# Weight sums of the seven-product pairs moved to GpSimd, part sums kept in PSUM, low parts merged

## The chip, the cores and the metric

The kernel runs on one core of a Trainium2 chip. The metric is the device time of one execution in microseconds, the median of several runs. The profile is of one further execution on the same core, taken by the hardware profiler.

## The reference

One inference step of a decoder trunk with two layers, on 576 tokens (64 sample tokens and 512 prompt tokens) of 1024 features. Each layer is a feed-forward block a, a token mixer (mLSTM in layer 0, gated linear attention in layer 1) and a feed-forward block b:

```python
x = x + 0.5 * swiglu(rmsnorm(x, norm_w[l, 0]), w_gate, w_up, w_down)
x = x + mixer(rmsnorm(x, norm_w[l, 1]))
x = x + 0.5 * swiglu(rmsnorm(x, norm_w[l, 2]), w_gate, w_up, w_down)

def swiglu(x, w_gate, w_up, w_down):
    return (silu(x @ w_gate) * (x @ w_up)) @ w_down
```

Everything is float32 in and out. The hidden width is 2816, that is 22 tiles of 128. The change touches the four feed-forward blocks.

## The kernel before

All features lie on partitions; x, the weights and the hidden rows are held in tiles of 128 features, and the 576 tokens are two halves of 288 columns (FIRST and SECOND). A float32 product is made on TensorE from three fp32r products, high times high, high times low and low times high. So each weight block that arrives by DMA in `raw` is rounded to `w_hi` by ScalarE (ACT), and VectorE (DVE) subtracts to make `w_lo`. `raw`, `w_hi` and `w_lo` have four slots of 1024 columns; a pair (a gate block and an up block for the same 128 hidden features) takes slots 0 and 1 or slots 2 and 3 (half 0 and half 1), and PSUM banks 0 to 3 or 4 to 7.

`schedule` (L35) lays out the phases. Each feed-forward block has three G phases (8, 8 and 6 pairs; `GROUPS`, L20), and each is followed by a D phase (4 pairs) that multiplies the hidden tiles by `w_down` and adds to x. In group 0 the first five pairs are plain: 96 matmuls of 288 columns each (`feature_pair`, L502). The last three pairs of group 0 and all pairs of groups 1 and 2 are seven-product pairs (`seven_pair`, L523): gate and up weights, over even and odd feature tiles, and the two token halves are taken as a two-by-two matrix product, which needs seven half-size products in place of eight, 84 matmuls. There are 17 such pairs in a block and 68 in all. The price is sums: of x (`th_hi`, `th_lo`, made once a block by `u_sums` L1895 and `t_sums` L1919), of weights (S1 to S4: `sum_3`, `sum_1`, `sum_2`, `sum_4`, L1771 to L1798, all on DVE), their high and low parts (`unit_high` L1198 and `unit_low` L1766, 512 columns each), and of products.

The products P1 to P7 of a pair run in a fixed order (L552 to L568). Product sums go like this before: ACT copies bank b+1 to SBUF after P1, P3 and P5 (`product_copy` L1217), and DVE adds these copies to banks in four steps (`part`, L1808), which leave the gate row in `T(0)` and bank b+1, and the up row in `T(1)`. Then come silu (L1252, L1254; in group 0 after a multiplication by `rstd`, `rows_scale` L1812, then L1257), the product of gate and up (`rows_product` L1822), and its high and low parts into `h_hi`, `h_lo`.

The order on each engine is written out by hand and each engine runs its instructions in order. On DVE the body of a seven-product pair w is `seven_pair` (L1842): between its own low parts and part sums it finishes the rows of pair w-1 and makes the weight sums of pair w+1. On ACT it is `seven_rest` (L1228) and `seven_rows` (L1246), which call `seven_start` (L1221) of the pair after. SyncE (SP) issues every weight load; the load of a slot waits on `lo_done` (L356), that is for the low part of what the slot held. GpSimd (POOL) has only small work in the mixers (L1710 to L1733).

`T(i)` is one of ten scratch rows of 576 columns. `bc` (L151) holds rows that the mixers broadcast. `own` makes DVE wait for its own last instruction.

## Time and profile before

| | |
|---|---|
| median of 3 runs | 2196.25 us (2194.16 to 2197.27) |
| span of the profiled execution | 2198.8 us |
| busy PE, DVE, ACT, POOL | 2160.5, 1555.5, 951.1, 45.7 us |
| matmuls | 16360, of which 5712 in seven-product pairs (L536) |
| chain that ended last | PE 91%, DVE 5%, ACT 2% |
| PE idle, from first to last matmul and before | some 29 us in gaps of over 0.05 us, 8.9 of it before the first matmul |

PE is TensorE's matmuls, PEld its weight loads, PEclk the granted clock in tenths of full speed. Matmuls are pipelined: a record of one lasts 0.29 us while they start some 0.13 us apart, so a stage is read by where it begins and ends, not by the busy time of a group. In a timeline, a record's end overlaps the start of the next on the same engine; the distance from start to start is what an instruction costs its engine.

### The profile page before, as it was taken

How to read it: one execution, taken by the hardware profiler on the slowest of the kernel's cores; microseconds unless marked ns; L12 is line 12 of the kernel's file. 1: busy time of each engine (PE TensorE's matmuls, PEld its weight loads, DVE VectorE, ACT ScalarE, POOL GpSimd, SP SyncE). 2: the span in 40 equal slices, each digit the busy share in tenths (PEclk: the TensorE clock that was granted, in tenths of full speed). 3: DMA queues.
4: the chain of work that ended last, by engine and by line, in shares of the span. 5: the costliest groups of instructions: out<-in, count | busy, mean ns of one | idle time of the engine just before them, and what ended most of it. 6: DMA issues, size and time to landing. Idle time of an engine off the chain costs nothing.

```text
span 2198.8 us, 40702 instructions
## 1 busy us (share of the span) xinstructions
PE 2160.5 (98%) x16360; PEld 2137.4 (97%) x16360; DVE 1555.5 (71%) x2379; ACT 951.1 (43%) x1495; POOL 45.7 (2%) x50
## 2 busy tenths in 40 slices
PE   7999999999999999999999999999999999999997
PEld 7999999999999999999999999999999899999997
DVE  6898657685555798848679984863776457988485
ACT  5435435454433444515445452544322434445252
POOL 0000000001100000000000000000011100000000
PEclk9999999999999999999999999999999999999999
DMA  5222322224332232222323232232122222223222
GB/s 186 68 88 95 115 67 86 96 82 137 99 118 85 68 102 82 95 87 89 104 70 94 86 96 96 82 101 94 44 96 84 97 77 84 90 87 104 77 86 73
DMA packets 72578, 201.58 MB, mean 92 GB/s; under 512 B 7268, under 2 KB 26980, under 8 KB 72448
## 3 DMA queue, kind: packets, MB, share of 16 engines
q1 hardware_dynamic: 72448, 199.80, 28.1%
q8 instruction: 88, 1.44, 0.3%
q14 instruction: 42, 0.34, 0.1%
HBM read 187.82 MB, written 11.95 MB: 91 GB/s over the span
## 4 chain that ended last, share of the span: by engine, by line
PE 91%; DVE 5%; ACT 2%; issue 1%; DMA 0%; POOL 0%; SPq 0%; DVEq 0%; POOLq 0%
PE ps L479 48%; PE ps L536 32%; PE ps L753 4%; PE ps L608 1%; DVE w_lo L1768 1%; PE ps L784 1%; PE ps L773 1%; PE ps L787 0%; DVE w_lo L1753 0%; PE ps L803 0%; PE ps L617 0%; PE ps L796 0%; PE ps L631 0%; PE ps L797 0%; DMA x<-in_x 0%
## 5 line engine op out<-in xcount | busy, mean ns | idle before, releaser
L479 PE MATMUL ps<-h_lo,w_hi 128*128 128x288 f32 x1616 | 347.0, 294 | 4.1 <-DVE h_hi L2267 4.1
L479 PE MATMUL ps<-h_hi,w_hi 128*128 128x288 f32 x1616 | 346.5, 294 | 0.7 <-DVE w_lo L1753 0.7
L536 PE MATMUL ps<-th_hi,w_hi 128*128 128x288 f32 x1088 | 320.2, 294 | 2.4 <-ACT scratch L1219 2.4
L536 PE MATMUL ps<-th_lo,w_hi 128*128 128x288 f32 x1088 | 320.9, 295 | 0.0
L536 PE MATMUL ps<-th_hi,w_lo 128*128 128x288 f32 x1088 | 319.8, 294 | 0.0
L479 PE MATMUL ps<-h_hi,w_lo 128*128 128x288 f32 x1360 | 290.2, 292 | 0.0
L479 PE MATMUL ps<-xn_hi,w_hi 128*128 128x288 f32 x1152 | 257.2, 300 | 11.6 <-DVE w_lo L1753 8.9
L479 PEld LDWEIGHTS ps<-h_lo,w_hi 128*128 128x128 f32 x1616 | 259.9, 188 | 4.8 <-DVE h_hi L2267 4.5
L479 PEld LDWEIGHTS ps<-h_hi,w_hi 128*128 128x128 f32 x1616 | 259.9, 188 | 1.0 <-DVE w_lo L1753 0.9
L1753 DVE TENSOR_TENSOR w_lo<-raw,w_hi 128x1024 fp32r<-128x1024 f32 x196 | 232.2, 1221 | 36.9 <-ACT w_hi L1185 35.1
L479 PE MATMUL ps<-xn_hi,w_lo 128*128 128x288 f32 x1152 | 251.9, 296 | 0.0
L479 PE MATMUL ps<-xn_lo,w_hi 128*128 128x288 f32 x1152 | 251.7, 296 | 0.0
L1768 DVE TENSOR_TENSOR w_lo<-scratch,w_hi 128x512 fp32r<-128x512 f32 x272 | 181.8, 690 | 84.8 <-ACT w_hi L1200 84.4
L1185 ACT ACTIVATE w_hi<-raw 128x1024 fp32r<-128x1024 f32 x196 | 195.8, 1047 | 105.2 <-PE ps L479 80.5
L536 PE MATMUL ps<-xn_hi,w_lo 128*128 128x288 f32 x816 | 240.4, 295 | 0.0
L536 PE MATMUL ps<-xn_hi,w_hi 128*128 128x288 f32 x816 | 239.9, 294 | 0.0
L536 PE MATMUL ps<-xn_lo,w_hi 128*128 128x288 f32 x816 | 239.9, 294 | 0.0
L479 PEld LDWEIGHTS ps<-h_hi,w_lo 128*128 128x128 f32 x1360 | 217.5, 187 | 0.0
L536 PEld LDWEIGHTS ps<-th_hi,w_hi 128*128 128x128 f32 x1088 | 204.8, 188 | 3.7 <-issue 3.2
L479 PEld LDWEIGHTS ps<-xn_hi,w_hi 128*128 128x128 f32 x1152 | 187.7, 190 | 19.9 <-issue 17.5
L2019 DVE SCALAR_TENSOR_TENSOR x<-ps,x 128x1152 f32<-128x1152 f32 x52 | 70.5, 1356 | 191.9 <-PE ps L479 191.9
L536 PEld LDWEIGHTS ps<-th_hi,w_lo 128*128 128x128 f32 x1088 | 204.4, 188 | 0.0
(288 smaller groups left out, 4119.7 us busy)
## 6 DMA issues: line engine op xcount, KB each, us to landing
raw<-in_w_gate SPq DMA_DIRECT2D x88, 512.0 KB, 3.4
raw<-in_w_up SPq DMA_DIRECT2D x88, 512.0 KB, 4.2
raw<-in_w_down SPq DMA_DIRECT2D x64, 512.0 KB, 3.6
raw<-in_w_mix SPq DMA_DIRECT2D x64, 512.0 KB, 4.2
raw<-in_w_down SPq DMA_DIRECT2D x32, 384.0 KB, 3.2
state_s<-in_state_c SPq DMA_DIRECT2D x4, 1024.0 KB, 7.5
out_c_s<-state_s SPq DMA_DIRECT2D x4, 1024.0 KB, 4.6
state_s<-in_state_g SPq DMA_DIRECT2D x4, 1024.0 KB, 6.1
```

Of the source, the lines that this page charges most:

```text
L479: ins = nc.tensor.matmul(o, a, b[:, c] if c is not None else b, start=first and j == 0, stop=last and j == 2)
L536: ins = nc.tensor.matmul(ps[:, bank, FIRST], left, b_, start=first and k == 0 and j == 0, stop=k == KT_X // 2 - 1 and j == 2, skip_group_c ...
L608: ins = nc.tensor.matmul(ps[:, bank, c * P:(c + 1) * P], left[:, ts], right[:, ts], start=True, stop=True)
L753: ins = nc.tensor.matmul(out, a[:, k, xs], b[:, 2 * half:2 * half + 2, ws], start=k == 0 and j == 0, stop=k == KT_X - 1 and j == 2)
L773: ins = nc.tensor.matmul(ps[:, 4 + c // 2, (c % 2) * DV:(c % 2 + 1) * DV], k_tok[:, c, :], v_tok[:, 1 + c, h * DV:(h + 1) * DV], start=Tru ...
L784: ins = nc.tensor.matmul(out, v_tok[:, 1 + c, vs], att(mixer, h)[:, c * P:(c + 1) * P], start=True, stop=c == 0)
L1185: nc.scalar.activation(w_hi[:, slot, :], raw[:, slot, :], ACT.Copy).then_inc(hi_done, 1)
L1753: V.tensor_tensor(w_lo[:, slot, :], raw[:, slot, :], w_hi[:, slot, :].bitcast(f32), ALU.subtract).then_inc(lo_done, 1)
L1768: return V.tensor_tensor(by_tile(unit(w_lo, half, u)), src, by_tile(unit(w_hi, half, u)).bitcast(f32), ALU.subtract)
L2019: ins = V.scalar_tensor_tensor(xs, ps[:, b:b + 4, 0:HALF_TOK], scale, xs, ALU.mult, ALU.add)
```

## The change

Weights. The host stores the gate and up weights of a pair so that four units of 512 columns lie one after the other: W12 and W11 (gate, odd and even feature tiles), then W21 and W22 (up, even and odd). The tensor `raw` now has two halves of 2624 columns, each with the first block, a free space of 576 columns and the second block. The space takes S3 in the feed-forward blocks and the rows of `bc` in the mixers. GpSimd makes S3 = W11 + W21 and S1 = W21 + W22 (the latter in place of W21), 128x512 each, for every seven-product pair (`weight_sums`); DVE makes S2 = S1 + W11 and S4 = W12 + S2. The high and the low parts of W11 and W12 are each made in one instruction of 1024 columns. S2 and S4 have scratch rows of their own for each half.

Products. P1 to P7 are the same seven products with 12 matmuls each; P4 now is W12's and P2 is S3's. ACT copies P1 into bank b, where P4 accumulates on it; DVE writes bank b+3 plus the copy of b+1 (after P3) into bank b+2, where P6 accumulates on it; one more DVE addition goes into bank b+3. So gate and up rows end as two banks each, and silu, the scaling by `rstd` and the row product read them with one instruction of 576 columns each.

Signs. The sums are arranged so that the up row comes out negated; plain pairs of group 0 negate theirs too, the result is added to x with -0.5, and the sums of x use negated weights (`neg_w`, four small DVE instructions at the start of the program) or a multiplication by -1.

Loads of group 0 are unrolled on SP. The loads, their sizes and the waits on `lo_done` stay. The core of the diff (left out: the same renaming in `split`, `mix` loads and late weights, the semaphore counts in `schedule`, and the host's code):

```diff
-        raw = sb("raw", [P, 4, KT_X * P])
+        raw = sb("raw", [P, 2, RAW_ALL])
...
+        neg_w = sb("neg_w", [P, 4, KT_X // 2])
+
+        def raw_slot(slot, n=KT_X * P):
+
+            at = RAW_UP if slot % 2 else 0
+            return raw[:, slot // 2, at:at + n]
+
+        def bc(i):
+
+            return raw[:, i, RAW_LOW:RAW_UP]
...
+        W12_AT, W11_AT, S3_AT, S1_AT, W22_AT = 0, UNIT, RAW_UP - UNIT, RAW_UP, RAW_UP + UNIT
+
+        def raw_unit(half, at):
+
+            return raw[:, half, at:at + UNIT]
+
+        def s2(half):
+
+            return T(8 + half)[:, 0:UNIT]
+
+        def s4(half):
+
+            return T(6 + half)[:, 0:UNIT]
+
+        U_W12, U_W11, U_S2, U_S3, U_S1, U_S4, U_W22 = 0, 1, 2, 3, 1, 2, 3
...
+                    return io["w_gu"][bass.ds(m, 1), :, s % 2 * 2 * UNIT:(s % 2 + 1) * 2 * UNIT]
...
-                pe.wait_ge(unit_lo, 5 * w + 1)
-                product(0, b + 1, x_tiles(even, 0), True).then_inc(product_done, 1)
                 pe.wait_ge(lo_done, 2 * pair + 1)
-                product(1, b, x_tiles(odd, 0), True).then_inc(product_done, 1)
-                pe.wait_ge(unit_lo, 5 * w + 2)
+                product(U_W11, b + 1, x_tiles(even, 0), True).then_inc(product_done, 1)
+                pe.wait_ge(unit_lo, 4 * w + 1)
+                product(U_S3, b + 3, t_tiles(2), True).then_inc(product_done, 1)
+                pe.wait_ge(unit_lo, 4 * w + 2)
                 pe.wait_ge(copy_done, 3 * w + 1)
-                product(2, b + 1, t_tiles(1), False).then_inc(product_done, 1)
-                pe.wait_ge(unit_lo, 5 * w + 3)
-                product(3, b + 2, t_tiles(2), True).then_inc(product_done, 1)
-                pe.wait_ge(unit_lo, 5 * w + 4)
+                product(U_S2, b + 1, t_tiles(1), False).then_inc(product_done, 1)
+                product(U_W12, b, x_tiles(odd, 0), False).then_inc(product_done, 1)
+                pe.wait_ge(unit_lo, 4 * w + 3)
                 pe.wait_ge(copy_done, 3 * w + 2)
-                product(0, b + 1, t_tiles(0), False).then_inc(product_done, 1)
+                product(U_S1, b + 1, t_tiles(0), False).then_inc(product_done, 1)
                 pe.wait_ge(lo_done, 2 * pair + 2)
-                product(1, b + 3, t_tiles(3), True).then_inc(product_done, 1)
-                pe.wait_ge(unit_lo, 5 * w + 5)
+                pe.wait_ge(part_ready, 2 * w + 1)
+                product(U_W22, b + 2, t_tiles(3), False).then_inc(product_done, 1)
+                pe.wait_ge(unit_lo, 4 * w + 4)
                 pe.wait_ge(copy_done, 3 * w + 3)
-                return product(2, b + 1, x_tiles(odd, 1), False)
+                return product(U_S4, b + 1, x_tiles(odd, 1), False)
...
-                unit_high(half, 0, raw_tiles(half, 0, 0)).then_inc(unit_hi, 1)
-                unit_high(half, 1, raw_tiles(half, 0, 1)).then_inc(hi_done, 1)
+                nc.scalar.activation(w_hi[:, 2 * half, :], raw_w(half), ACT.Copy).then_inc(hi_done, 1)
 
             def sums_high(ph, i, half):
 
                 w = ph["seven"] + 2 * i + half
-                act.wait_ge(sum_ready, 4 * w + 3)
-                unit_high(half, 2, by_tile(S2)).then_inc(unit_hi, 1)
-                unit_high(half, 3, by_tile(S3)).then_inc(unit_hi, 1)
+                act.wait_ge(sums_full[half], sums_at(ph, i, half))
+                unit_high(half, U_S3, raw_unit(half, S3_AT)).then_inc(unit_hi, 1)
+                act.wait_ge(sum_ready, 2 * w + 1)
+                unit_high(half, U_S2, s2(half)).then_inc(unit_hi, 1)
...
-                product_copy(P1_COPY, half)
-                unit_high(half, 0, by_tile(S1)).then_inc(unit_hi, 1)
+                product_copy(ps[:, 4 * half, FIRST], half)
+                unit_high(half, U_S1, raw_unit(half, S1_AT)).then_inc(unit_hi, 1)
...
                 act.wait_ge(product_done, 6 * w + 2)
-                act.wait_ge(raw_full[2 * half + 1], 8 * (pair - half) + 16)
-                unit_high(half, 1, raw_tiles(half, 1, 1)).then_inc(hi_done, 1)
+                unit_high(half, U_W22, raw_unit(half, W22_AT)).then_inc(hi_done, 1)
+                if not last:
+                    weights_high(ph, *step(i, half))
                 act.wait_ge(product_done, 6 * w + 3)
                 product_copy(U2_COPY, half)
-                unit_high(half, 2, by_tile(S4)).then_inc(unit_hi, 1)
+                act.wait_ge(sum_ready, 2 * w + 2)
+                unit_high(half, U_S4, s4(half)).then_inc(unit_hi, 1)
                 if not last:
-                    weights_high(ph, *step(i, half))
+                    sums_high(ph, *step(i, half))
                 act.wait_ge(product_done, 6 * w + 5)
                 product_copy(U4_COPY, half)
                 if last:
                     split(PHASES[j + 1], 0, 0)
-                else:
-                    sums_high(ph, *step(i, half))
...
-                    act.wait_ge(part_ready, 4 * w + 1)
-                    nc.scalar.activation(T(0)[:, FIRST], T(0)[:, FIRST], ACT.Silu)
                     act.wait_ge(pe_done, pair + 1)
-                    nc.scalar.activation(T(0)[:, SECOND], ps[:, 4 * half + 1, FIRST], ACT.Silu).then_inc(gate_done, 1)
+                    nc.scalar.activation(cut2(T(0)), ps[:, b:b + 2, FIRST], ACT.Silu).then_inc(gate_done, 1)
...
+            def weight_sums(ffn):
+
+                for ph in PHASES:
+                    if ph["kind"] != "G" or ph["ffn"] != ffn:
+                        continue
+                    for m in range(ph["skip"], ph["pairs"]):
+                        i, half, pair = m // 2, m % 2, ph["base"] + m
+                        pool.wait_ge(raw_full[2 * half + 1], 8 * (pair - half) + 16)
+                        if ph["group"] == 0:
+                            pool.wait_ge(rstd_ready, ph["norm"] + 1)
+                        pool.wait_ge(raw_full[2 * half], 8 * (pair - half) + 16)
+                        G.tensor_tensor(raw_unit(half, S3_AT), raw_unit(half, W11_AT), raw_unit(half, S1_AT), ALU.add)\
+                            .then_inc(sums_full[half], 8)
+                        pool.wait_ge(sums_full[half], sums_at(ph, i, half) - 8)
+                        G.tensor_tensor(raw_unit(half, S1_AT), raw_unit(half, S1_AT), raw_unit(half, W22_AT), ALU.add)\
+                            .then_inc(sums_full[half], 8)
+
+            weight_sums(0)
             for u in range(2 * N_HEADS):
 
+                if u == N_HEADS:
+                    weight_sums(1)
+                    weight_sums(2)
...
+            def sum_2(ph, i, half):
 
                 pair = ph["base"] + 2 * i + half
-                for blk in range(2):
-                    dve.wait_ge(raw_full[2 * half + blk], 8 * (pair - half) + 16)
-                V.tensor_tensor(by_tile(S3), raw_tiles(half, 0, 0), raw_tiles(half, 1, 0), ALU.subtract)\
-                    .then_inc(sum_ready, 1)
-
-            def sum_1(ph, i, half):
+                dve.wait_ge(raw_full[2 * half], 8 * (pair - half) + 16)
+                dve.wait_ge(sums_full[half], sums_at(ph, i, half))
+                V.tensor_tensor(s2(half), raw_unit(half, S1_AT), raw_unit(half, W11_AT), ALU.add).then_inc(sum_ready, 1)
+
+            def sum_4(ph, i, half):
+
+                dve.wait_ge(sum_ready, 2 * (ph["seven"] + 2 * i + half) + 1)
+                V.tensor_tensor(s4(half), raw_unit(half, W12_AT), s2(half), ALU.add).then_inc(sum_ready, 1)
+
+            def weights_low(ph, i, half):
+
+                dve.wait_ge(hi_done, 2 * (ph["base"] + 2 * i + half) + 1)
+                V.tensor_tensor(w_lo[:, 2 * half, :], raw_w(half), w_hi[:, 2 * half, :].bitcast(f32), ALU.subtract)\
+                    .then_inc(lo_done, 1)
...
+                m, b = 2 * i + half, 4 * half
                 dve.wait_ge(pe_done, ph["base"] + m + 1)
-                V.tensor_tensor(T(0)[:, SECOND], ps[:, 4 * half + 1, FIRST], rstd[:, SECOND], ALU.mult)\
-                    .then_inc(gate_ready, 1)
-                V.tensor_tensor(T(1), T(1), rstd[:, :], ALU.mult).then_inc(up_ready, 1)
+                V.tensor_tensor(cut2(T(0)), ps[:, b:b + 2, FIRST], cut2(rstd[:, :]), ALU.mult).then_inc(gate_ready, 1)
+                dve.wait_ge(part_ready, 2 * (ph["seven"] + m) + 2)
+                V.tensor_tensor(cut2(T(1)), ps[:, b + 2:b + 4, FIRST], cut2(rstd[:, :]), ALU.mult).then_inc(up_ready, 1)
...
-                V.tensor_tensor(T(2), T(0), T(1), ALU.mult).then_inc(psum_free, 1)
+                    up = cut2(T(1))
+                V.tensor_tensor(cut2(T(2)), cut2(T(0)), up, ALU.mult).then_inc(psum_free, 1)
...
                 if before and ph["group"] == 0:
                     rows_scale(ph, *before)
                 if not last:
-                    dve.wait_ge(unit_lo, 5 * w + 3)
-                    sum_3(ph, *after)
+                    sum_2(ph, *after)
                 if before:
                     rows_product(ph, *before)
-                dve.wait_ge(sum_ready, 4 * w + 4)
-                dve.wait_ge(unit_hi, 5 * w + 4)
-                unit_low(half, 0, by_tile(S1)).then_inc(unit_lo, 1)
+                if not last:
+                    sum_4(ph, *after)
+                dve.wait_ge(unit_hi, 4 * w + 3)
+                unit_low(half, U_S1, raw_unit(half, S1_AT)).then_inc(unit_lo, 1)
                 if before:
                     rows_low(ph, *before)
                 dve.wait_ge(hi_done, 2 * pair + 2)
-                unit_low(half, 1, raw_tiles(half, 1, 1)).then_inc(lo_done, 1)
-                dve.wait_ge(copy_done, 3 * w + 1)
+                unit_low(half, U_W22, raw_unit(half, W22_AT)).then_inc(lo_done, 1)
+                if not last:
+                    weights_low(ph, *after)
+                dve.wait_ge(copy_done, 3 * w + 2)
                 dve.wait_ge(product_done, 6 * w + 2)
-                part(T(0)[:, FIRST], half, 0, P1_COPY)
-                dve.wait_ge(unit_hi, 5 * w + 5)
-                unit_low(half, 2, by_tile(S4)).then_inc(unit_lo, 1)
-                if not last:
-                    dve.wait_ge(unit_lo, 5 * w + 4)
-                    sum_1(ph, *after)
-                    sum_2(ph, *after)
-                dve.wait_ge(copy_done, 3 * w + 2)
-                dve.wait_ge(product_done, 6 * w + 4)
-                part(T(4)[:, SECOND], half, 2, U2_COPY)
-                if not last:
-                    dve.wait_ge(unit_lo, 5 * w + 5)
-                    sum_4(ph, *after)
-                dve.wait_ge(copy_done, 3 * w + 3)
-                part(T(1)[:, SECOND], half, 2, U4_COPY)
+                V.tensor_tensor(ps[:, b + 2, FIRST], ps[:, b + 3, FIRST], U2_COPY, ALU.add).then_inc(part_ready, 1)
+                dve.wait_ge(unit_hi, 4 * w + 4)
+                unit_low(half, U_S4, s4(half)).then_inc(unit_lo, 1)
                 if last:
                     split(PHASES[j + 1], 0, 0, (0,))
                 else:
                     sums_low(ph, *after)
-                dve.wait_ge(product_done, 6 * w + 6)
-                dve.wait_ge(part_ready, 4 * w + 2)
-                part(T(1)[:, FIRST], half, 3, T(4)[:, SECOND])
+                dve.wait_ge(copy_done, 3 * w + 3)
+                V.tensor_tensor(ps[:, b + 3, FIRST], ps[:, b + 3, FIRST], U4_COPY, ALU.add).then_inc(part_ready, 1)
                 if last:
                     split(PHASES[j + 1], 0, 0, (1,))
...
-                own(V.tensor_tensor(T(5)[:, SECOND], odd[:, SECOND], T(5)[:, FIRST], ALU.subtract))
-                V.tensor_tensor(T(6)[:, SECOND], odd[:, FIRST], T(5)[:, SECOND], ALU.subtract).then_inc(t_ready, 1)
+                own(V.scalar_tensor_tensor(T(5)[:, SECOND], odd[:, SECOND], -1.0, T(5)[:, FIRST], ALU.mult,
+                                           ALU.subtract))
+                V.scalar_tensor_tensor(T(6)[:, SECOND], odd[:, FIRST], -1.0, T(5)[:, SECOND], ALU.mult,
+                                       ALU.subtract).then_inc(t_ready, 1)
...
-                    add_to_x(ph, pp, 0.5, final=ph["last"])
+                    add_to_x(ph, pp, -0.5, final=ph["last"])
...
+                    for ffn, norm in enumerate((0, 2, 3, 5)):
+                        V.tensor_scalar(neg_w[:, ffn, :], norm_w[:, norm, 1::2], -1.0, None, ALU.mult)
```

## Rows read from the trace of the kernel before

**Rows 1.** The page: busy time, and the granted clock in 40 slices.

```profile
PE 2160.5 (98%) x16360; PEld 2137.4 (97%) x16360; DVE 1555.5 (71%) x2379; ACT 951.1 (43%) x1495; POOL 45.7 (2%) x50
...
PEclk9999999999999999999999999999999999999999
```

**Rows 2.** The chain in order of time, L536's long pieces: start, us, what.

```profile
164.97 88.80 PE ps L536 x672
...
761.87 4.79 PE ps L536 x36
776.86 19.46 PE ps L536 x144
```

**Rows 3.** What PE waited for, whole span: us in total, times, longest.

```profile
PE ps L536 <- ACT scratch L1219: 2.4, 4, 0.7
```

**Rows 4.** Timeline around one stall: start, us, engine, line, tiles [idle before, releaser].

```profile
776.86 0.37 PE L536 MATMUL ps<-th_hi,w_hi 128*128 128x288 f32 x1 [0.66 <-ACT scratch L1219]
...
775.73 0.69 ACT L1257 ACTIVATE scratch<-scratch 128x576 f32<-128x576 f32 x1 [3.21 <-DVE scratch L1818]
776.32 0.39 ACT L1219 ACTIVATE scratch<-ps 128x288 f32<-128x288 f32 x1
```

**Rows 5.** Timeline of ACT in a steady pair that starts at 187.17.

```profile
195.12 0.41 ACT L1219 ACTIVATE scratch<-ps 128x288 f32<-128x288 f32 x1 [1.20 <-PE ps L536]
```

**Rows 6.** Timeline of DVE in the same pair: W22's low part; and SP's load after.

```profile
191.14 0.69 DVE L1768 TENSOR_TENSOR w_lo<-raw,w_hi 128x512 fp32r<-128x512 f32 x1
...
191.86 0.33 SPq L357 DMA_DIRECT2D raw<-in_w_up  x1
```

**Rows 7.** DMA issues by line, 164 to 254: count, KB, median us to landing.

```profile
raw<-in_w_up SPq DMA_DIRECT2D x6, 512.0 KB, 3.4
```

**Rows 8.** The same from 115 to 165, where two loads are issued close together.

```profile
raw<-in_w_gate SPq DMA_DIRECT2D x2, 512.0 KB, 3.4
raw<-in_w_up SPq DMA_DIRECT2D x2, 512.0 KB, 4.4
```

**Rows 9.** Groups of DVE and ACT, shapes apart: busy us, mean ns | idle before.

```profile
L1753 DVE TENSOR_TENSOR w_lo<-raw,w_hi 128x1024 fp32r<-128x1024 f32 x196 | 232.2, 1221 | 36.9 <-ACT w_hi L1185 35.1
L1768 DVE TENSOR_TENSOR w_lo<-scratch,w_hi 128x512 fp32r<-128x512 f32 x272 | 181.8, 690 | 84.8 <-ACT w_hi L1200 84.4
L1810 DVE TENSOR_TENSOR scratch<-ps,scratch 128x288 f32<-128x288 f32 x272 | 123.5, 454 | 18.1 <-ACT scratch L1219 18.1
L1831 DVE TENSOR_TENSOR scratch<-scratch 128x576 f32<-128x576 f32 x68 | 51.5, 757 | 1.7
...
L1200 ACT ACTIVATE w_hi<-scratch 128x512 fp32r<-128x512 f32 x272 | 163.7, 626 | 44.2 <-DVE scratch L1790 44.2
```

**Rows 10.** Groups of POOL: its two-input instructions.

```profile
L1733 POOL TENSOR_TENSOR scratch<-scratch 128x576 f32<-128x576 f32 x8 | 11.5, 1440 | 133.6 <-ACT scratch L1452 93.2 <-ACT scratch L1446 40.4
L1718 POOL TENSOR_TENSOR vs_lo<-v_tok,vs_hi 64x256 fp32r<-64x256 f32 x8 | 6.4, 801 | 250.1 <-ACT vs_hi L1462 250.1
```

**Rows 11.** Timelines of POOL and DVE in the second mixer, from 1590.

```profile
1590.57 4.78 POOL L1729 TENSOR_TENSOR k_tok_b<-k_hl,cst 128x1024 fp32r<-128x1024 f32 x1
...
1591.24 2.35 DVE L1753 TENSOR_TENSOR w_lo<-raw,w_hi 128x1024 fp32r<-128x1024 f32 x2
```

**Rows 12.** The same from 1636.

```profile
1636.67 1.90 POOL L1729 TENSOR_TENSOR k_tok_b<-k_hl,cst 128x1024 fp32r<-128x1024 f32 x1
...
1636.84 2.34 DVE L2432 TENSOR_TENSOR qt<-qt,bc 128x576 f32<-128x576 f32 x1
```

**Rows 13.** Timeline of DVE at the end of the D phase of group 0, block 0.

```profile
159.43 0.68 DVE L1776 TENSOR_TENSOR scratch<-raw 128x512 f32<-128x512 f32 x1
...
163.16 1.28 DVE L1768 TENSOR_TENSOR w_lo<-scratch,w_hi 128x512 fp32r<-128x512 f32 x2
```

**Rows 14.** DVE groups of x sums, plain and with a scalar: mean ns.

```profile
L1901 DVE SCALAR_TENSOR_TENSOR scratch<-x,norm_w,scratch 128x288 f32<-128x288 f32 x16 | 8.3, 519 | 0.6
L1931 DVE TENSOR_TENSOR scratch<-scratch 128x288 f32<-128x288 f32 x16 | 7.2, 451 | 0.0
```

144 lines of the change are left out of this document (71 added, 73 removed).

## The prediction

> **What bounds the kernel now.** I read the page first: PE is busy 98% of the span at the full granted clock, DVE 71%, ACT 43%, POOL 2% [rows 1]. A busy PE is not proof of a bound, so I read the chain in order of time: in it the eight seven-product pairs of a group 1 are one unbroken piece of 672 matmuls in 88.80 us [rows 2]. That is 132.1 ns a matmul and 11.10 us a pair, with no gap in which anything else ended last. Then I asked what PE waited for. In the stages that the change touches one entry is left, ACT's copy of a product (L1219): 2.4 us in 4 times [rows 3]. The timeline of one of them shows it: in group 0, PE stops before the third product of a pair, because ACT copies P1 only after the silu of the pair before, and that silu waited 3.21 us for DVE, which reached its scaling (L1816, L1818) late, behind four part sums and eight low parts [rows 4]. The matmul count is the same before and after, so nearly all of the 2198.8 us stays, unless a wait appears; the change can only take away such stalls, or make new ones.
>
> **The stall that goes.** From P1 of the first seven-product pair of group 0 (761.87) to the first matmul of the D phase (776.86 + 19.46 = 796.32) pass 34.45 us for 252 matmuls [rows 2]. At 132.1 ns these are 33.30 us, so 1.15 us are lost: 0.66 idle and the restart of the pipeline, and a smaller wait a pair later. The four blocks do this alike (in block 0 it is 0.8), in all 0.8 + 3 x 1.15 = 4.2 us. After the change the gate needs one scaling of 576 columns straight from PSUM. With t as time from the start of a pair, the pair ends at 11.10, the scaling takes 0.75 us like L1831 [rows 9], silu 0.69 [rows 4], so ACT is free at 12.65; P1 of the next pair ends at 11.10 + 1.59 = 12.69, and its copy (0.4 us) is done by 13.15, before P3 starts at 14.27. That stall goes, if DVE is there in time.
>
> **DVE, steady pair.** Removed: two sums of 512 columns, two part sums, and one instruction of two low parts. An instruction of 512 columns costs 0.60 from start to start (0.69 long), 1024 1.14, 576 0.67, 288 from PSUM 0.37 [rows 9]. Before: 10 x 0.60 + 2 x 0.67 + 4 x 0.37 = 8.8 us of 11.10; after: 7 x 0.60 + 1.14 + 2 x 0.67 + 2 x 0.37 = 7.4 us. The order by time: S2 of the next pair, row product (after silu, t 0.75), S4, S1's low part (S1's high part follows the copy of P1 and is ready at 2.6, ACT taking 0.63 [rows 9]), rows' low part, W22's low part ending at 4.7, the merged low part of W11 and W12 ending at 6.2, the part sum ending at 6.6, S4's low part 7.2, S3's and S2's 8.4, and the last part sum after ACT's copy of P5, that starts at 195.12 - 187.17 = 7.95 [rows 5], so 8.9.
>
> **The new wait of PE** is P6 on the part sum in PSUM: needed at 5 x 1.586 = 7.93, ready at 6.6. Spare 1.3 us; cost nothing in the steady pairs. In the first seven-product pair of group 0, DVE comes from a plain pair: two readings of PSUM, their product, rows' low part, then S2, S4, two low parts, the merged one, and the part sum. Added up from the plain pair's end: 1.4 to the product, its rounding on ACT, low part at 3.2, then 0.67 + 0.70 + 4 instructions (0.6, 0.6, 1.14, 0.45): 8.0 us. That is at the edge of 7.93. I take 0.2 us of wait a block, 0.8 in all; ends 0 and 0.6 a block.
>
> **GpSimd.** The trace before has no 128x512 sum on POOL. Its nearest are 1.44 us for 128x576 and 0.80 for 64x256 [rows 10]; by the slope, 0.0020 us a column, 512 columns are 1.3 us, bounds 0.8 and 1.9. Two a pair, one after the other, 2.7 us with the semaphore between. W22's low part ends at 191.83 and SP's load of the up block goes out 0.03 later [rows 6], t 4.7; alone it lands in 3.4 us, and the first of two loads 1 us apart still does, the second in 4.4 [rows 7, 8]. The merged low part moves the gate load forward to t 6.2, that is 1.5 us behind the up load, so the up load stays first. It lands at 8.2, and the two sums run from 8.3 to 11.0. DVE needs S1 at 11.10 for S2: just in time, and S1's low part waits for ACT until 13.7 anyway, so 0.6 more hurts nobody. The loop from W22's low part to the next one is load 3.5 + sums 2.7 + S2, row product, S4, three low parts 3.9 = 10.1 us, and must stay under 11.10: spare 1.0, or 0.5 a sum.
>
> **Sharing between DVE and GpSimd.** The rows show that these two engines block one another: a POOL instruction that takes 1.90 us alone took 4.78 while DVE ran two-input instructions back to back, and elsewhere a DVE instruction of 0.74 us took 2.34 because POOL had started 0.17 earlier [rows 11, 12]. In the steady pair POOL's 8.3 to 11.0 falls into DVE's idle time, with only a part sum in it that reads one operand from PSUM. The Trainium skill, SBUF — State Buffer, section Who interferes with whom, says that a DVE instruction with two SBUF inputs contends with a GpSimd instruction that reads SBUF, that the later one blocks fully, and that one with at most one SBUF input does not contend; the first half agrees with rows 11 and 12, and by the second the part sum is free. If that rule held without the idle time, all of the 2.7 us would fall on DVE (7.4 + 2.7 = 10.1, still under 11.10).
>
> **D phase of group 0.** Here DVE is full with the sums of x. Before, the weight sums and low parts start at 159.43 and end at 164.44 [rows 13], PE starts on the next group at 164.97 [rows 2]. After, PE's first product needs S2, S4 and the merged low part: 0.72 + 0.60 + 1.22 = 2.5 us, ready at 162.0, 3.0 us spare. From this goes 0.5 for eight sums of x that become scalar_tensor_tensor (0.519 against 0.451 [rows 14]) and the blocking by four POOL sums (two pairs are loaded in this phase). Their loads go out after a pair's low parts, so each pair's first sum meets the sums of x, 1.3 us, and its second falls beside the addition to x, which reads PSUM. I take 2.6 us; ends 0 and 5.2. So the wait is 2.6 + 0.5 - 3.0 = 0.1 us a block, 0.4 in all; ends 0 and 2.7 a block. Groups 1 and 2: DVE is mostly idle in their D phases, no cost.
>
> **The rest, at nothing.** The four neg_w instructions (4 columns each) stand ahead of the first low part; 288 columns cost 0.37 [rows 9], so four are under 1.5 us and I take 0.3. DVE waits for ACT soon after, and that idle time takes it up; if not, it costs that. Negation in plain pairs: the same 0.75. Unrolled loads: the same waits. The tail (last D phase) has its DVE chain unchanged from ACT's copies on. The mixers only get `bc` at another address.
>
> **Sum.** -4.2 + 0.8 + 0.4 + 0 = -3.0 us: 2198.8 becomes 2195.8 in a profiled execution. The median before is 2.55 below its profiled span, so 2193.2 for the median.
>
> **Rivals.** (1) The stall is only moved: P6 in group 0 costs what P3 did (0.6 a block), or the scaling is late again, and D-phase waits eat the rest. For it: at 8.0 against 7.93 the path is at its edge, and each pause of PE costs a restart of some 0.2 to 0.5. -4.2 + 2.4 + 1.6 = -0.2: 2196. (2) Slower: in the D phase of group 0 all four POOL sums block DVE, or are themselves held and then block it at a worse place. Decides from 2.5 us of blocking on; at 5.2 it is 2.7 a block, 10.8 in all: 2196.3 - 4.2 + 0.8 + 10.8 = 2203.7. For it: rows 11 and 12 and a DVE without idle time there; against: each pair's second sum should meet the addition to x. By the skill's rule just named this case is what full blocking gives. (3) Much slower: in steady pairs a POOL sum takes over 1.8 us, the loop passes 11.10 and every one of some 60 pairs pays. At the 4.78 of rows 11, a pair gains 2.9 us, the loop is 13.0, and the time 2196 + 60 x 1.9 = 2310. Against it: POOL starts when DVE goes idle. A mild form (one blocked sum a pair, 0.2 over) is 2208. (4) Faster still: PE's pace. Matmuls of plain pairs start 130.0 ns apart and seven-product ones 132.1, with no wait in either; the change moves tensors and the order of products, and 0.5 ns on 5712 is 2.9 us either way; with both stalls gone altogether, 2190.
>
> **Chances.** Forecast 0.50 (own range 2191 to 2196), rival 1 0.20, rival 2 0.13, rival 3 0.07 (mostly mild), rival 4 0.10. A difference of 0.2%, 4.4 us, is about what a measurement can tell from no change. Faster by more (under 2191.9): rival 4 and the lower part of the forecast, 0.22. Slower by more: rivals 2 and 3 and a little of 1, 0.20. Within: 0.58. Range 2189 to 2203: it leaves out rival 3, part of rival 2 and the far end of 4.
>
> **What the profile after would show.** POOL some 136 instructions more, of 1.3 us; PE with no wait on a copy of P1 in group 0 (34.45 down to 33.4 to 33.6 us); group 1 still 88.80 us; DVE down some 1.4 us a pair, 95 in all; S2 starting at t 0.1 of a pair; at the start of group 1 a PE wait of 0 to 0.3 us. The prediction is wrong if group 1 takes over 89 us, if DVE's 512-column instructions show a mean well over 0.69, or if PE waits for a low part at 165.

## The result

The changed kernel takes 2209.21 us (median of 4 runs, 2208.22 to 2210.47), the kernel before 2196.75 us (2194.16 to 2197.27) beside it: a ratio of 1.006, 95% interval 1.0045 to 1.0074. It is slower by 12.5 us, where 3.0 us less than the 2196.25 then known was forecast (2193.2, range 2189 to 2203). The profiled execution spans 2208.2 us against 2198.8, so 9.4 us are to be found in the two traces.

The page of the changed kernel, busy time of each engine and the granted clock:

```profile
PE 2171.4 (98%) x16360; PEld 2148.8 (97%) x16360; DVE 1436.5 (65%) x2031; ACT 937.9 (42%) x1371; POOL 236.1 (11%) x186
...
PEclk9999999999999999999999999999999999999998
```

Beside [rows 1]: the same 16360 matmuls, the same clock but for the last slice, and DVE has lost 119 us. But PE is busy 10.9 us longer. TensorE hardly waits more; it works longer on the same work. What it waits for says so too (us in total, times, longest; the first six entries and one later):

```profile
PE ps L525 <- DVE w_lo L1821: 10.2, 2, 9.5
PE ps L525 <- DVE h_hi L2306: 4.1, 2, 2.1
PE ps L1165 <- DVE scratch L2627: 3.7, 1, 3.7
PE ps L655 <- DVE raw L2492: 2.2, 1, 2.2
PE ps L525 <- issue: 1.9, 1, 1.9
PE ps L850 <- POOL scratch L1800: 1.7, 4, 1.1
...
PE ps L583 <- DVE ps L1916: 0.7, 4, 0.2
```

The 2.4 us of [rows 3] are gone and four waits of 0.2 us for the part sum have come; of the others only the first has grown, by 0.7 us (9.5 before, most of it at the start of the program). So nearly all of the loss has to be in stretches without waits. The chain, in order of time (start, us, what; L583 is a seven-product pair, L525 all others, L525 x384 behind L583 a down phase):

```profile
81.28 1.60 PE ps L583 x12
...
89.39 25.64 PE ps L583 x192
115.04 51.19 PE ps L525 x384
166.22 88.87 PE ps L583 x672
255.09 51.19 PE ps L525 x384
...
372.93 57.52 PE ps L525 x432
...
712.57 50.18 PE ps L525 x384
```

and the same pieces of the kernel before (there L479 for L525; group 1 is in [rows 2]):

```profile
115.06 49.92 PE ps L479 x384
...
253.78 49.92 PE ps L479 x384
370.30 56.45 PE ps L479 x432
...
711.69 50.18 PE ps L479 x384
```

There it is: the 384 matmuls of a down phase take 51.19 us instead of 49.92, 133.3 ns each instead of 130.0, without a gap in either. The seven-product pairs (88.87 against 88.80) and the plain pairs of group 0 (50.18 in both) are as before. Eleven of the twelve down phases are affected; the last one, which stops for a wait and has other spacings, takes 39.31 us for its 288 in both traces.

| where | before | after | times | in all |
|---|---|---|---|---|
| down phase, 384 matmuls | 49.92 | 51.19 | 8 | +10.2 |
| down phase, 288 matmuls | 37.44 | 38.39 | 3 | +2.9 |
| group 0, 252 matmuls (block 0) | 34.11 | 33.75 | 1 | -0.4 |
| group 0, 252 matmuls (later blocks) | 34.45 | 33.75 | 3 | -2.1 |
| groups 1 and 2 | 88.80, 66.60 | 88.87, 66.65 | 4 each | +0.5 |

That is 11.1 us. The start, one group of plain pairs and the second mixer add 0.3 to 0.4 us each, and the first mixer, whose TensorE work the change leaves alone, took 2.7 us less. So the 9.4 of the spans come out. The last stage of that mixer, before and after, and in a run told of below (one wait less in a pair):

```profile
654.55 56.16 PE ps L479 x408
```

```profile
656.73 54.86 PE ps L525 x408
```

```profile
655.44 54.65 PE ps L525 x408
```

Two things differ here. The first is the granted clock in 3.4 us at the start of the stage (start and end, length, busy us of PE, PEld, DVE, ACT and POOL with counts in brackets, granted clock, share and rate of DMA), after and in that run:

```profile
656.70:660.10 3.40, 3.37 (x14) 3.37 (x15) 1.54 (x4) 0.00 (x0) 0.00 (x0) 0.50 0.26 89
```

```profile
655.44:658.84 3.40, 3.40 (x25) 3.40 (x26) 1.51 (x4) 0.00 (x0) 0.00 (x0) 1.00 0.27 92
```

At 0.50, the lower level of 1.2 GHz, matmuls start 240 ns apart; the stretch costs some 1.5 us (56.16 against 54.65). TensorE had stood waiting for DVE just ahead of it. But the same wait comes with and without such a stretch: the trace of before has five of them between the first and the last matmul (at 41.3, 474.8, 655.7, 1635.3 and 1748.0 us), that of after four, that of the other run none. The second is the pace behind it: 130.0 ns a matmul after, 133.3 before and in every other run here. The 40-slice row of the page shows neither.

Other engines show nothing that could be the cause. The window from 373 to 428 us lies in the group-2 down phase and the first matmuls of the mixer behind it, in both traces (columns as above). Before, then after:

```profile
373.00:428.00 55.00, 55.00 (x422) 55.00 (x421) 28.75 (x28) 20.06 (x24) 0.00 (x0) 1.00 0.29 98
```

```profile
373.00:428.00 55.00, 55.00 (x415) 55.00 (x414) 30.31 (x29) 21.45 (x25) 0.00 (x0) 1.00 0.33 106
```

GpSimd does nothing in either, DVE is idle nearly half the time, the clock is full, and TensorE starts 415 matmuls where it started 422.

One step finer, the times from one matmul's start to the next, read from the trace at the second of these down phases. The bar is the phase's entry. Nanoseconds:

```
                   last 8 starts of the pair ahead       | first 12 of the down phase
before, 253.6 us   132 132 133 136 132 132 133 136       | 126 132 128 132 128 132 128 132 128 132 128 132
after,  254.9 us   132 133 136 132 132 133 136 133       | 130 133 129 133 132 133 131 130 132 131 131 140
```

The quick down phase repeats after two (132, 128), the slow one after four (131, 131, 132, 140). And the last product of a seven-product pair repeats after four too, with one long start of 135 or 136. Before, that long one is the last ahead of the entry; after, it is the last but one. I call this the place: 1 before, 2 after. It is the same at all eleven entries of each trace.

### The profile page after: what moved, and what is told of

Same layout as the page of the kernel before. It is cut to its first block, busy times and chain, and to the rows that moved or that the text cites. A ratio compares the mean times of both kernels' runs of the same rounds, so it can differ in the third digit from the quotient of the medians.

```text
span 2208.2 us, 40072 instructions
## 1 busy us (share of the span) xinstructions
PE 2171.4 (98%) x16360; PEld 2148.8 (97%) x16360; DVE 1436.5 (65%) x2031; ACT 937.9 (42%) x1371; POOL 236.1 (11%) x186
## 4 chain that ended last, share of the span: by engine, by line
PE 93%; DVE 4%; ACT 2%; issue 1%; DMA 0%; POOL 0%; SPq 0%; DVEq 0%; POOLq 0%
PE ps L525 49%; PE ps L583 33%; PE ps L800 4%; PE ps L655 1%; PE ps L831 1%; PE ps L820 1%; DVE w_lo L1821 1%; PE ps L834 0%; PE ps L850 0%; PE ps L664 0%; DMA x<-in_x 0%; PE ps L678 0%; PE ps L843 0%; PE ps L844 0%; DVE x L2641 0%
## 5 line engine op out<-in xcount | busy, mean ns | idle before, releaser
L525 PE MATMUL ps<-h_lo,w_hi 128*128 128x288 f32 x1616 | 351.4, 297 | 4.1 <-DVE h_hi L2306 4.1
L525 PE MATMUL ps<-h_hi,w_hi 128*128 128x288 f32 x1616 | 351.1, 296 | 0.7 <-DVE w_lo L1821 0.7
L583 PE MATMUL ps<-th_hi,w_hi 128*128 128x288 f32 x1088 | 320.9, 295 | 0.7 <-DVE ps L1916 0.7
L583 PE MATMUL ps<-th_hi,w_lo 128*128 128x288 f32 x1088 | 321.2, 295 | 0.0
L583 PE MATMUL ps<-th_lo,w_hi 128*128 128x288 f32 x1088 | 320.4, 294 | 0.0
L525 PE MATMUL ps<-h_hi,w_lo 128*128 128x288 f32 x1360 | 295.1, 296 | 0.0
L525 PE MATMUL ps<-xn_hi,w_hi 128*128 128x288 f32 x1152 | 257.4, 301 | 11.7 <-DVE w_lo L1821 9.5
L525 PEld LDWEIGHTS ps<-h_lo,w_hi 128*128 128x128 f32 x1616 | 262.6, 189 | 4.8 <-DVE h_hi L2306 4.5
L525 PEld LDWEIGHTS ps<-h_hi,w_hi 128*128 128x128 f32 x1616 | 262.6, 189 | 1.0 <-DVE w_lo L1821 0.9
L525 PE MATMUL ps<-xn_lo,w_hi 128*128 128x288 f32 x1152 | 252.1, 296 | 0.0
L525 PE MATMUL ps<-xn_hi,w_lo 128*128 128x288 f32 x1152 | 252.0, 296 | 0.0
L583 PE MATMUL ps<-xn_hi,w_lo 128*128 128x288 f32 x816 | 240.1, 294 | 0.0
L583 PE MATMUL ps<-xn_hi,w_hi 128*128 128x288 f32 x816 | 239.8, 294 | 0.0
L583 PE MATMUL ps<-xn_lo,w_hi 128*128 128x288 f32 x816 | 239.7, 294 | 0.0
L1767 POOL TENSOR_TENSOR raw<-raw 128x512 f32<-128x512 f32 x68 | 93.5, 1375 | 1318.8 <-DMA raw<-in_w_gu 1294.9
L525 PEld LDWEIGHTS ps<-h_hi,w_lo 128*128 128x128 f32 x1360 | 220.4, 189 | 0.0
L525 PEld LDWEIGHTS ps<-xn_hi,w_hi 128*128 128x128 f32 x1152 | 187.9, 190 | 20.0 <-issue 18.2
L583 PEld LDWEIGHTS ps<-th_hi,w_hi 128*128 128x128 f32 x1088 | 204.5, 188 | 1.6 <-issue 1.6
L583 PEld LDWEIGHTS ps<-th_lo,w_hi 128*128 128x128 f32 x1088 | 204.6, 188 | 0.0
```

What stands on the lines that cost most here:

```text
L525: ins = nc.tensor.matmul(o, a, b[:, c] if c is not None else b, start=first and j == 0, stop=last and j == 2)
L583: ins = nc.tensor.matmul(ps[:, bank, FIRST], left, b_, start=first and k == 0 and j == 0, stop=k == KT_X // 2 - 1 and j == 2, skip_group_c ...
L1767: G.tensor_tensor(raw_unit(half, S3_AT), raw_unit(half, W11_AT), raw_unit(half, S1_AT), ALU.add)\
```

## The experiments

Each is a single profiled execution, unless an interval is given. "Down piece" is the chain's row of 384 matmuls at 253 to 258 us; the kernel before is timed beside it on the same chip. Such a time holds none to six of the 1.5 us stretches at the lower clock, so the down pieces decide and the times only go along.

### Memory addresses

The changed `raw` takes in `bc`, so that all weight and hidden tensors lie 4608 bytes further on. Two kernels: the one before with `bc` moved,

```diff
         raw = sb("raw", [P, 4, KT_X * P])
+        bc = sb("bc", [P, 2, TOK])
...
-        bc = sb("bc", [P, 2, TOK])
```

> The kernel before with one line moved: the two broadcast rows bc are allocated right behind raw, so that w_hi, w_lo, h_hi and h_lo lie 4608 bytes further on, as they do in the changed kernel. No instruction is changed. Theory A (the addresses of the weights and the hidden tensor set TensorE's pace in the down phases): the down stretches of 384 matmuls go from 49.92 to 51.19 us, the time from 2196.7 to 2209 to 2211. Theory B (what TensorE does and waits for in the pairs ahead of a down phase sets it): 49.92 and 2196 to 2198, as before. Theory C (other engines' traffic disturbs it): as B.

and the changed one with `raw` behind `scratch`.

```diff
-        raw = sb("raw", [P, 2, RAW_ALL])
...
         scratch = sb("scratch", [P, 10, TOK])
+        raw = sb("raw", [P, 2, RAW_ALL])
```

> The changed kernel with raw allocated behind scratch instead of ahead of w_hi: w_hi, w_lo, h_hi, h_lo and the hidden halves all lie 20992 bytes lower than in the changed kernel, and 16384 lower than in the kernel before. No instruction is changed. Theory A: some other pace, most likely 49.92 us for 384 matmuls of a down phase and 2195 us. Theory B and C: 51.19 us and 2209 us, as the changed kernel.

The first: 2200.07 us beside 2199.88. The second: 2208.92 beside 2199.88. Their chains:

```profile
253.78 49.92 PE ps L479 x384
```

```profile
255.37 51.19 PE ps L525 x384
```

Each keeps its own pace at the other's addresses or at quite different ones. Addresses of the weights and hidden tensors are out.

### Waits of the pair

The sixth product now waits on two semaphores. One wait less after, one more before:

```diff
-                pe.wait_ge(lo_done, 2 * pair + 2)
                 pe.wait_ge(part_ready, 2 * w + 1)
```

> The changed kernel, but the sixth product of a seven-product pair waits for one semaphore instead of two: the wait for the low part of W22 is left out, since VectorE makes it ahead of the part sum that the product waits for anyway. Theory B: the pattern of starts in the pair changes, and with it possibly the pace that a down phase falls into: 49.92 us for 384 matmuls and 2194 to 2197 us if it falls into the quick one; if it stays at 51.19 and 2209 the pace is not set by this wait. Theory A and C: 51.19 us and 2209 us.

```diff
+                pe.wait_ge(const_in, CONST_ALL)
                 product(1, b + 3, t_tiles(3), True).then_inc(product_done, 1)
```

> The kernel before, with one more wait ahead of the sixth product of each seven-product pair, on a semaphore that has been met since the start (the constants' loads). Nothing waits longer for data. Theory B: the place and number of waits sets the pace of the down phase, so 51.19 us for 384 matmuls and 2206 to 2210 us; if this place is not the one that counts, 49.92 and 2197. Theory A and C: 49.92 us and 2196 to 2197 us.

Down pieces 51.19 and 49.92, times 2204.83 and 2198.86 beside 2199.88. The pattern of starts over the seven products is the old one in both to within 1 ns or 2, and the place is 2 and 1 as it was. So the number of waits, where they are met, isn't it. The 2204.83 is lower than 2209 for another reason: this is the execution without a stretch at the lower clock, where the changed kernel's trace has four, 6.0 us. (One of them is the difference between 38.62 and 40.12 us for a run of 288 matmuls in block 0.)

### Extra matmuls at the entry

Ahead of the loop of each down phase, one, two or three matmuls that the next one overwrites:

```diff
+                    if ph["kind"] == "D":
+                        pe.wait_ge(psum_free, ph["base"] - 1)
+                        pe.wait_ge(lo_done, 2 * ph["base"] + 1)
+                        pe.wait_ge(hl_ready, ph["hidden"] - 1)
+                        for _ in range(1):
+                            nc.tensor.matmul(ps[:, 0, 0:HALF_TOK], w_hi[:, 0, 0:P], h_hi[:, 0, 0:HALF_TOK],
+                                             start=True, stop=True)
```

> The kernel before with one extra matmul at each of the 12 down phases' entries. B1: the phase is entered one place later in TensorE's cycle, and can fall from the quick pace (49.92 us for 384 matmuls) into the slow one (51.19): 2210 to 2213 us if so, else 2198 to 2200. B2: 49.92 us and 2198 to 2200 us.

> The changed kernel with one matmul more (128x128 weights, 288 columns, overwritten by the next one into that bank) at the entry of each of the 12 down phases. In the slow pace the starts repeat after four matmuls (131, 131, 132, 140 ns), in the quick one after two (132, 128). Theory B1 (the pace is set by where in TensorE's own cycle of four the down phase is entered): one, two or three extra matmuls at the entry move that place, and at least one of the three numbers brings the quick pace: 12 phases hold 8x384 + 4x288 = 4224 matmuls at 3.3 ns less, 14.1 us, against 12x0.13 = 1.6 us for the extra ones: 2196 to 2198 us with one extra. Theory B2 (the pace comes from the code of the pair before, wherever the phase is entered): 51.19 us for 384 matmuls and 2210 to 2211 us for each number.

> As the run with one extra matmul at each down phase's entry, with two. B1: 2197 to 2200 us if this number brings the quick pace, 2212 if not; B2: 2212 us and 51.19 us for 384 matmuls.

> As the run with one extra matmul at each down phase's entry, with three. B1: 2199 to 2201 us if this number brings the quick pace, 2214 if not; B2: 2214 us.

The kernel before falls: 2212.85 us beside 2198.86, with

```profile
254.73 51.33 PE ps L479 x384
```

where the unchanged one has 49.92. So 14.0 us, more than the change lost, come from eleven matmuls (1.5 us of work, and over 1 us in the stalls told of below) put into the old kernel. (The expectations count twelve phases and 14.1 us; it is eleven and 13.1.) The changed kernel stays slow with one, two and three: 2211.01, 2213.76, 2212.87, down pieces of 51.2 to 51.3. By the expectation, one of the three should have been quick. But with one extra matmul, in either kernel, the added waits also put a stall of some 0.1 us or more at each of the eleven entries (in the kernel before, at 254 us, starts of 185 and 207 ns where 132 is usual), so these two runs move two things at once. With two extra it stands at two of the eleven entries only, and with three at none (130 134 132 127 135 at 254 us): there the matmuls alone were added, and the slow pace stayed. Another form without a wait doubles the first matmul of each two-pair iteration and adds no wait:

```diff
+                            if ph["kind"] == "D" and slot == 0 and k == 0:
+                                nc.tensor.matmul(out[0][0], w_hi[:, slot, ws], xh[:, k, out[0][1]],
+                                                 start=True, stop=True)
```

> The changed kernel with the first matmul of each two-pair iteration of the down phases issued twice (24 matmuls more, 3.2 us, the second overwrites the first), with no wait added: unlike the earlier runs with extra matmuls it moves the place in the cycle and inserts no stall. B1: 49.92 us for 384 matmuls and about 2198 us if one place is what is missing; otherwise 51.19 and 2212 us.

2212.66 us beside 2197.12, 133.3 ns a matmul at all eleven entries. The place, counted at the last matmul of the pair, was still 2. So in the changed kernel matmuls added behind the entry don't bring the quick pace. Whether the matmul or its stall slowed the kernel before isn't separated by these runs.

### The order of the streamed sources

Before, the seven products stream x x t t t t x (x: tiles of x, t: token sums), after x t t x t t x. Exchanged in both:

```diff
-                product(1, b, x_tiles(odd, 0), True).then_inc(product_done, 1)
+                product(1, b, t_tiles(2), True).then_inc(product_done, 1)
...
-                product(3, b + 2, t_tiles(2), True).then_inc(product_done, 1)
+                product(3, b + 2, x_tiles(odd, 0), True).then_inc(product_done, 1)
```

> The kernel before, where in each seven-product pair the second and the fourth product exchange the data that they stream: the second reads the halves of the token sums (t_tiles) and the fourth the odd tiles of x. That changes what is computed (two of the seven products get each other's operand) and leaves weights, banks, waits and counts alone. The order of sources becomes x t t x t t x, as in the changed kernel, instead of x x t t t t x. B3 (the order of the sources in the pair carries TensorE's cycle of starts to another place by the end of the pair, and so the down phase into the slow pace): 51.19 us for 384 matmuls of a down phase, 2208 to 2212 us. B4 (waits, banks or accumulation flags do): 49.92 us and 2196 to 2199 us.

> The changed kernel, where in each seven-product pair the second and the fourth product exchange the data that they stream (two of the seven products get each other's operand, so the result is another), giving the sources the order of the kernel before, x x t t t t x. B3: the down phases go back to 49.92 us for 384 matmuls, the time to 2194 to 2197 us. B4: 51.19 us and 2209 us.

The exchange gives two products each other's operand, so these two kernels compute something else; weights, waits and counts are the same. Half of B3 holds. The kernel before goes slow with this alone: 2212.51 us beside 2197.12, and its place is 4 at ten entries. At the eleventh it is 1, and that phase alone is quick. The chain of this one kernel, same code in each phase:

```profile
800.23 49.92 PE ps L479 x384
850.15 89.00 PE ps L536 x672
939.15 51.20 PE ps L479 x384
```

The starts ahead of the two entries end in 132 132 133 136 at 800 us, and in 136 133 131 134 at 939. The other half falls: the changed kernel with the old order stays at place 2 and at 51.19 (2212.26 us). The new order can cause the slow pace, but its undoing isn't enough; something else of the new pair takes part, and whether that is its banks, its accumulation or its unit slots was not tested.

Two edits of the same kind that moved nothing: another order of the three terms in the seventh product (2213.28 us beside 2197.12, place 2),

```diff
-                        for j, (left, b_) in enumerate(((wh, xh), (wh, xl), (wl, xh))):
+                        terms = ((wh, xh), (wl, xh), (wh, xl)) if low_first else ((wh, xh), (wh, xl), (wl, xh))
+                        for j, (left, b_) in enumerate(terms):
```

> The changed kernel with the three terms of the seventh product in another order (low part of the weights second instead of third): same matmuls, same sum. If the place in the cycle at the end of the pair is what counts, this may move it: 49.92 us for 384 matmuls of a down phase and 2194 to 2197 us; if it doesn't, 51.19 and 2209. No wait is changed, so nothing between these two is expected.

and the two column halves of the down phases in the other order (2209.53 beside 2198.37, place 2).

```diff
+                    both = (1, 0) if ph["kind"] == "D" else (0, 1)
-                    for cs in ((0,), (1,)) if by_bank and blk == 1 else ((0, 1),):
+                    for cs in ((0,), (1,)) if by_bank and blk == 1 else (both,):
```

> The changed kernel with the two column halves of each weight tile in the down phases taken in the other order: same matmuls, same count, no wait changed. Place theory: the entry's place is not moved, so slow, 51.19 us for 384 matmuls and 2209 us, unless the other half at the start makes up for one place; then 49.92 and 2195, which would be a version ahead of both kernels.

### The place itself

By now place 1 had always been quick and places 2 and 4 slow. To move the place and nothing else, matmuls are added inside the seventh product, that need no wait: low part times low part, for the first three or one of its four tiles.

```diff
-                        for j, (left, b_) in enumerate(((wh, xh), (wh, xl), (wl, xh))):
+                        terms = [(wh, xh), (wh, xl), (wl, xh)] + ([(wl, xl)] if k < low_low else [])
+                        for j, (left, b_) in enumerate(terms):
```

> The changed kernel with three matmuls more in the seventh product (the product of the low parts, for three of its four tiles: it belongs to the exact product and only adds a term near rounding; its operands are there, so no wait is added and no stall). Place theory (every quick down phase so far is entered right behind the long one, 135 or 136 ns, of the last product's cycle of four starts; in the changed kernel the long one comes last but one, so the entry is one place late, and three more bring it round): 49.92 us for 384 matmuls of a down phase, and 2209 + 68x3x0.132 - 14.1 = 2222 us. Rival (the code or the order of sources sets the pace, not the place): 51.19 us, 2236 us.

> The changed kernel with one such matmul more in the seventh product. Place theory: the long start is then last but two at the entry, so the phase stays slow: 51.19 us for 384 matmuls, 2209 + 9 = 2218 us. If the pace came back to 49.92 here too (2204 us), the place theory would be wrong: any disturbance would do.

> The kernel before with one such matmul more in the seventh product, with no wait and no stall (the earlier run with one more matmul at the down phase's entry put a stall there as well). Place theory: the long start is no longer the last ahead of the entry, 51.19 us for 384 matmuls, 2197 + 9 + 14 = 2220 us. Rival (the change of order or waits is needed): 49.92 us, 2206 us.

Chains of the three, in this order:

```profile
165.54 92.06 PE ps L584 x696
257.60 49.92 PE ps L525 x384
376.56 56.45 PE ps L525 x432
```

```profile
165.15 90.03 PE ps L584 x680
255.17 51.20 PE ps L525 x384
```

```profile
165.43 89.87 PE ps L537 x680
255.30 51.19 PE ps L479 x384
```

and their starts around that entry:

```
after + 3    133 136 133 131 134 136 | 125 132 128 132 128     place 1, quick
after + 1    136 132 132 133 136 133 131 | 132 131 131 140     place 3, slow
before + 1   132 133 136 132 132 133 136 133 | 130 133 129     place 2, slow
```

All three as the place theory said, at all eleven entries of each. The changed kernel has its quick down phases back with three extra matmuls in a pair and not with one, so it isn't that any disturbance helps; the old kernel loses them with one, with no stall put in. The times, 2226.61, 2219.24 and 2221.37 beside 2198.37, hold 27.0, 9.0 and 9.0 us for the added matmuls; 2222, 2218 and 2220 were expected. The first is 4.6 over: 1.0 is the 14.1 of the expectation that should be 13.1, and in its trace the granted clock is 0.50 for 20 us in all, against 14 in the changed kernel's, which is 3.0 us.

Over the fifteen kernels here that put nothing in at the entry there are 165 entries: the 56 quick ones all have a start of 135 or 136 last, the 109 slow ones none (88 have it last but one, 11 last but two, 10 last but three).

### Giving it back

One try without extra work: the seventh product's first matmul issued ahead of the sixth's last, so that eleven instead of twelve follow the last streamed token sum.

```diff
-                product(U_W22, b + 2, t_tiles(3), False).then_inc(product_done, 1)
+                product(U_W22, b + 2, t_tiles(3), False, range(11))
                 pe.wait_ge(unit_lo, 4 * w + 4)
                 pe.wait_ge(copy_done, 3 * w + 3)
-                return product(U_S4, b + 1, x_tiles(odd, 1), False)
+                product(U_S4, b + 1, x_tiles(odd, 1), False, range(1))
+                product(U_W22, b + 2, t_tiles(3), False, (11,)).then_inc(product_done, 1)
+                return product(U_S4, b + 1, x_tiles(odd, 1), False, range(1, 12))
```

> The changed kernel with no matmul more: the first matmul of the seventh product is issued ahead of the last one of the sixth, so that eleven instead of twelve in a row follow the last that streams a token sum (another order of the same terms). Place theory: eleven are one place less, which is the same as three more, so the down phases come back to 49.92 us for 384 matmuls, and the time to 2209.2 - (8x1.27 + 4x1.1) = 2195 us, range 2193 to 2198; the seventh product's two waits come one matmul earlier, which may add up to 0.1 us in the pairs that wait for them. If the cycle doesn't start anew where the source changes, the pace stays at 51.19 and the time at 2209 us.

2209.17 us (5 runs), ratio to the kernel before 1.0057, interval 1.0043 to 1.0071; place 2, 51.19. The cycle doesn't begin anew where the source changes: the number of matmuls moves the place, their order here didn't.

The other pays the three matmuls only where they count, in the last pair ahead of eleven down phases, which is written out behind the loop:

```diff
-                return product(U_S4, b + 1, x_tiles(odd, 1), False)
+                return product(U_S4, b + 1, x_tiles(odd, 1), False, 3 if seam else 0)
...
+                    peel = ph["kind"] == "G" and ph["hidden"] + ph["pairs"] < HIDDEN_ALL
-                    with pe.Fori(0, ph["pairs"] // 2) as i:
+                    with pe.Fori(0, ph["pairs"] // 2 - peel) as i:
                         iteration(i, seven=(0, 1) if ph["kind"] == "G" else ())
+                    if peel:
+                        iteration(ph["pairs"] // 2 - 1, seven=(0, 1), seam=True)
```

> The changed kernel with the three extra matmuls in the seventh product of only the last pair ahead of a down phase, at 11 of the 12 entries (the last one is left as it is): 33 matmuls more, 4.4 us. The last two pairs of a group are written out behind the loop for that. Place theory, with the place set inside the pair and not carried over from the pairs before: 49.92 us for 384 matmuls at the eight long down phases, 8x1.27 + 3x0.96 = 13.0 us less, so 2209.2 - 13.0 + 4.4 = 2200.6 us, range 2198 to 2203: slower than the kernel before by 0.2%, and quicker than the changed one by 0.4%. If the place is carried over from pair to pair: 51.19 us and 2213 us.

```profile
770.09 26.04 PE ps L584 x195
796.13 49.92 PE ps L525 x384
846.05 89.25 PE ps L584 x675
935.30 49.92 PE ps L525 x384
985.22 67.04 PE ps L584 x507
1052.26 49.91 PE ps L525 x384
```

2199.12 us (median of 11 runs) beside 2197.32 (15 runs): ratio 1.0007, interval 0.9998 to 1.0016. All eleven phases are quick. Against the changed kernel's 2209.2 that is 10.1 us back for 4.4 us of added work, and it can't be told from the kernel before. So extra matmuls in the last pair are enough. That the place isn't added up over the pairs is shown by the runs with one and with three in every pair: their groups have 3, 8 and 6 seven-product pairs, and the place is the same behind each. No version here is quicker than the kernel before.

## Why the prediction was wrong, step by step

- **The stall of group 0.** -4.2 and +0.8 forecast, -3.4 together; measured 3 x -0.70 and -0.36, -2.5. The copy's stall is gone and the new wait is the 0.2 us a block that was taken. Missed is the restart: 252 matmuls at 132.2 ns are 33.33 us, the stretch takes 33.75, and of the 0.42 only 0.18 is the wait. The removed stall was priced with its restart, the added one without. The 0.2 itself was luck: the terms of the prediction's sum for the part sum add up to 7.4 us, not to the 8.0 that it gives, and measured are 8.0 (the pair starts at 762.75):

```profile
770.25 0.46 DVE L1916 TENSOR_TENSOR ps<-ps,scratch 128x288 f32<-128x288 f32 x1
770.85 0.37 PE L583 MATMUL ps<-th_hi,w_hi 128*128 128x288 f32 x1 [0.18 <-DVE ps L1916]
```

- **Steady pairs.** No new wait, as forecast: 88.87 against 88.80. GpSimd's sums took 1.38 and 1.40 us on average against 1.3 forecast, inside the spare 0.5 each; 118 of the 136 took 1.25 to 1.35, and most of the longer ones met DVE instructions in group 0's down phase (see below):

```profile
L1770 POOL TENSOR_TENSOR raw<-raw 128x512 f32<-128x512 f32 x68 | 95.1, 1399 | 10.0 <-POOL raw L1767 0.4
L1767 POOL TENSOR_TENSOR raw<-raw 128x512 f32<-128x512 f32 x68 | 93.5, 1375 | 1318.8 <-DMA raw<-in_w_gu 1294.9 <-issue 23.9
```

- **DVE's work.** 95 us less forecast, 119 measured. I counted from start to start (0.60 an instruction), the page adds up lengths (0.69): a slip in what was compared, without effect on the time.
- **GpSimd against DVE in group 0's down phase.** 0.4 us of wait forecast, none came. The blocking is there; here the low parts of the token sums before and after (mean ns behind the busy time):

```profile
L1938 DVE TENSOR_TENSOR th_lo<-scratch,th_hi 128x1152 fp32r<-128x1152 f32 x16 | 21.7, 1359 | 0.6
```

```profile
L1981 DVE TENSOR_TENSOR th_lo<-scratch,th_hi 128x1152 fp32r<-128x1152 f32 x16 | 29.6, 1848 | 0.6
```

  The mean hides two kinds: eight of the 16 took 1.36 us as before, and eight, two in each block, 2.33 to 2.34. One of these, with what GpSimd did:

```profile
144.71 1.35 DVE L1977 TENSOR_TENSOR xn_lo<-scratch,xn_hi 128x1152 fp32r<-128x1152 f32 x1
146.10 2.34 DVE L1981 TENSOR_TENSOR th_lo<-scratch,th_hi 128x1152 fp32r<-128x1152 f32 x1
148.36 1.34 DVE L2062 SCALAR_TENSOR_TENSOR x<-ps,x 128x1152 f32<-128x1152 f32 x1
```

```profile
144.76 2.46 POOL L1767 TENSOR_TENSOR raw<-raw 128x512 f32<-128x512 f32 x1 [50.45 <-DMA raw<-in_w_gu]
147.36 2.23 POOL L1770 TENSOR_TENSOR raw<-raw 128x512 f32<-128x512 f32 x1
```

  Whoever starts second is held: GpSimd's first sum, begun 0.05 us behind a DVE instruction of 1.35 us, took 2.46, and the DVE instruction that began inside it took 1.0 us longer. That is 1.96 us a block, against 2.6 taken: it fits into the spare 3.0. The addition to x, which reads PSUM and one operand in SBUF, took its 1.34 us with GpSimd's second sum beside it, as forecast. That agrees with the Trainium skill, SBUF — State Buffer, section Who interferes with whom, by which a DVE instruction with at most one input in SBUF, outside the two-port modes, does not contend with GpSimd.
- **The start.** Under 0.3 us was taken; the pairs behind the first two stalls of the start begin 0.36 later (41.16 against 40.80).
- **The step that failed** is the sentence that since the matmul count is the same, nearly all of the 2198.8 us stays unless a wait appears. It holds only if a matmul's price is fixed. Rival 4 said that it isn't, named both paces, 130.0 and 132.1, and then allowed 0.5 ns on 5712 matmuls, 2.9 us either way, in the seven-product pairs alone, and gave the chance of it to the faster side. It was 3.3 ns on 3936 others, the down phases, and a loss: 13.1 us. The trace of before had the size of the step in it: in the last stage of the first mixer 336 matmuls in a row start 133.3 ns apart, in the down phases 130.0, the same kind of matmul with no wait in either. And the plain pairs of block 0 start 133.3 ns apart too (240 matmuls in 32.0 us from 48.78), where the prediction gives 130.0 for all plain pairs. I read past both, because the stages stood in the chain as unbroken pieces.
- **The test named for a wrong prediction** (group 1 over 89 us, long DVE instructions, a PE wait at 165) would not have caught it: none of these happened. Each asked for a wait or a contention.

The parts that I had priced come to -2.0 us (-2.5 for group 0, +0.5 for groups 1 and 2), near the -3.0 forecast; the term priced at nothing is +13.1.
